# Two low parts made before the last gated columns of each feed-forward layer, and unread products in four waits of the attention layers

## The chip, the core and the metric

The kernel runs on one core of a Trainium2 chip. A core has a matrix engine (TensorE, "PE" in the rows; its weight loads are "PEld"), a vector engine (VectorE, "DVE"), a scalar engine (ScalarE, "ACT"), a general engine (GpSimd, "POOL") and a queue engine (SyncE, "SP") that here only issues transfers. Each engine works through its own list of instructions in order and waits on semaphores that others raise. The metric is the device time of one execution in microseconds (us); lower is better.

## The reference, cut to what matters

A model of twelve layers works on 256 tokens of width 1024, in float32. The layers stand in this order: ffn0, sb (stick-breaking attention), ffn1, ffn2, mla (latent attention), ffn3, ssm, peer0, ple0, swa (windowed attention with shared keys), peer1, ple1. The change touches the four feed-forward layers and the entries of two attentions:

```python
def swiglu(x, w_in, w_out):                    # ffn0 to ffn3
    gate, up = jnp.split(x @ w_in, 2, axis=-1)
    return (jax.nn.silu(gate) * up) @ w_out    # 1024 -> 2816 (gate and up) -> 1024

def multi_head_latent_attention(...):          # mla
    proj = h @ w_in                            # 1024 -> 416
    q = (rms_norm(c_q, q_norm) @ w_uq)         # 256 -> 1536, part of it rotated
    kv = (rms_norm(c_kv, kv_norm) @ w_ukv)     # 128 -> 2048
    ...                                        # causal softmax attention, 16 heads

def swa_sink_attention(...):                   # swa
    q = apply_partial_rope(h @ q_w + q_b, cos, sin)
    ...                                        # windowed softmax attention, 16 heads
```

## The kernel before

**Numbers in two parts.** A float32 product is made of three products of rounded numbers: each operand is split into a high part and a low part (what rounding left over), and `products` (lines 473 to 475) adds high x high, high x low and low x high. The weights come as a stream of blocks of 128 x 1024 numbers into a ring of four places (`ring`, issued on SP's queue, L420). For each block ACT makes the high part (`make_hi`, L310, into `ring_hi`, four slots) and DVE or POOL the low part (`make_lo`, L316, into `ring_lo`). `make_hi` of block b waits until the block has landed and until PE has used block b-4, which had the same slot. The place in the ring is free for block b+4 once the low part of b is made.

**A feed-forward layer** has 66 blocks, numbered here from the layer's first. The hidden width 2816 is 22 columns of 128. For each column c PE multiplies one block of gate and one of up (`up(c)`), ACT takes the silu of the gate (`silu(c)`, L1139), and DVE multiplies and splits it (`hidden(c)`: w_hi L1681, L1682, w_lo L1684). The down blocks of columns 0 to 17 stand among the others. The last six gate and up blocks are 56 to 61, so that `up(21)` is blocks 60 and 61, and the last four down blocks are 62 to 65. They are worked off by `last_row_blocks`: for the first 128 tokens it goes through 62, 63, 64, 65 (six products of 512 columns each), then twice more through all four for the other tokens. Before a block it waits for its low part and for `hidden` of its column (18 to 21). The order on ACT and DVE at this place is written out by hand, and it is the same in all four layers: ACT makes the high parts of 60, 61, 62, then `silu(20)`, then 63, then `silu(21)`, then 64 and 65; DVE makes the low parts of 60 and 61, `hidden(20)`, low part of 62, `hidden(21)`, then the low parts of 63, 64, 65. After the layer `add_normed` (DVE) and `statistics` (ACT) take the sum out of PSUM, norm it and go on to the next layer: each layer begins with the result of the one before.

**Unread products.** `unread_products(n)` (L453) is a row of n float32 products of 128 x 128 with the identity, into an unused corner of PSUM that nobody reads. Before the change it is called with 7 and with 8 in the waits at the entry of the layers (`transposes_of_x`).

**mla** (L720 on): PE multiplies the four blocks of mla_in, then waits for `mla_cn` (ACT copies the product and sums squares, POOL takes the root, DVE scales, L1827); six transposes (L742); a wait for their copy out of PSUM in two parts (ACT L1278, DVE L1833); then 36 products for q, 24 for k and v; a wait for `mla_kv_d` (DVE copies and rotates q, then copies k and v, L1850); then the attention: for every pair of heads a turning of q (L661, in swa L664), scores (L678, L679), softmax on DVE and ACT, a turning of the weights (L688), values (L704). **swa** has the same attention; before it PE turns the keys (L797) and waits for `swa_q` (DVE adds a bias to q and rotates it, L1880).

Of the kernel before, what the change touches and what calls it, by code (L numbers as in the profile page):

```python
# [14 lines left out]
P = 128  # L15
# [5 lines left out]
FC = FF // P  # L21
# [120 lines left out]
def build_program(nc, stream, experts, x_in, pos_in, cols_in, rows_in, out):  # L142
    n_blocks = AT["end"]
    ctx = ExitStack()
    with ctx:
# [287 lines left out]
        def _(pe):  # L433
            ident = col("ident")
# [16 lines left out]
            def unread_products(n):  # L451
                for _ in range(n):
                    pe.matmul(ps[:, 7, 3 * P:4 * P], ident, col("ones"), start=True, stop=True)  # L453
# [270 lines left out]
            def mla():  # L724
# [3 lines left out]
                for k in range(KD):  # L728
                    b = base + k // 2
                    if k % 2 == 0:  # L730
                        wait_split(pe, b)
                    wait_hT(NORM_OF["mla"], k)
                    for tb in range(TB):
                        last = products(ps[:, tb, 0:MLA_IN], h_tiles(k, tb),
                                        ring_parts(b, slice((k % 2) * MLA_IN, (k % 2 + 1) * MLA_IN)),
                                        k == 0, k == KD - 1)
                    if k % 2:
                        last.then_inc(used, 1)
                pe.wait_ge(of("mla_cn"), 1)
# [4 lines left out]
                last.then_inc(of("mla_cT"), 1)  # L744
                pe.wait_ge(of("mla_cTs"), 1)
# [27 lines left out]
                pe.wait_ge(of("mla_kv_a"), 1)  # L773
                pe.wait_ge(of("mla_kv_d"), 1)
                attention(0, R)

            def swa():
# [20 lines left out]
                last.then_inc(of("swa_kT"), 1)  # L798
                pe.wait_ge(of("swa_q"), 1)
# [248 lines left out]
        def _(act):  # L1048
# [83 lines left out]
            def ffn(f, name):  # L1132
# [21 lines left out]
                for c, blocks in ((18, (54, 55, 56)), (19, (57, 58, 59)), (20, (60, 61, 62)), (21, (63,))):  # L1154
                    for b in blocks:
                        make_hi(act, base + b)
                    act.wait_ge(used, base + 3 * FC - TAIL - 2 * (FC - 1 - c) if c > 18 else base + 55)
                    act.wait_ge(hidden_ready, done + c - 1)
                    silu(c).then_inc(silu_ready, 1)
                for b in range(3 * FC - 2, 3 * FC):  # L1160
                    make_hi(act, base + b)
# [386 lines left out]
        def _(dve):  # L1548
# [123 lines left out]
            def ffn(f, name):  # L1672
# [27 lines left out]
                for c, blocks in ((18, (54, 55, 56)), (19, (57, 58, 59)), (20, (60, 61)), (21, (62,))):  # L1700
# [5 lines left out]
                for b in range(3 * FC - 3, 3 * FC):  # L1706
                    make_lo(dve, base + b)
# [678 lines left out]
```

## Time and profile before

| | us |
|---|---|
| median of 3 runs | 2895.51 (2893.81 to 2896.94) |
| the profiled execution, its own time | 2896.59 |
| its span in the trace | 2894.7 |
| PE busy (87% of the span) | 2505.3 |
| DVE busy (60%) | 1727.1 |
| ACT busy (41%) | 1189.8 |
| POOL busy (33%) | 963.2 |

The span is what the trace covers; 1.9 us of the execution lie outside of it. The layers before peer0 take the first 1325 us or so. "Granted clock" is the share of TensorE's full clock that the chip lets through: it is 1.00 (2.4 GHz) or 0.50 (1.2 GHz), and a value between the two is a mean over a stretch that saw both. Matmuls overlap: one of 512 columns lasts 0.39 us in a row of equals, and the next one starts after 0.23 us, so costs are read from starts and not from durations.

### The profile page before, as it was taken

How to read it: one execution, taken by the hardware profiler on the slowest of the kernel's cores; microseconds unless marked ns; L12 is line 12 of the kernel's file. 1: busy time of each engine (PE TensorE's matmuls, PEld its weight loads, DVE VectorE, ACT ScalarE, POOL GpSimd, SP SyncE). 2: the span in 40 equal slices, each digit the busy share in tenths (PEclk: the TensorE clock that was granted, in tenths of full speed). 3: DMA queues.
4: the chain of work that ended last, by engine and by line, in shares of the span. 5: the costliest groups of instructions: out<-in, count | busy, mean ns of one | idle time of the engine just before them, and what ended most of it. 6: DMA issues, size and time to landing. Idle time of an engine off the chain costs nothing.

```text
span 2894.7 us, 35382 instructions
## 1 busy us (share of the span) xinstructions
PE 2505.3 (87%) x12108; PEld 1782.7 (62%) x12108; DVE 1727.1 (60%) x3508; ACT 1189.8 (41%) x2574; POOL 963.2 (33%) x745
## 2 busy tenths in 40 slices
PE   8999899999889999996888787778886888877787
PEld 8988799899769988985444333333664444333334
DVE  5552255655455555785676767665456666676663
ACT  4346543434454356543333322333462333223333
POOL 0015400000320027665544333333534444433343
PEclk9999999999999999998999999999988999999999
DMA  6543255455415544436999999998428999999994
GB/s 210 187 165 124 95 185 192 161 191 180 140 59 182 186 157 139 146 106 241 418 416 419 421 420 418 421 414 331 136 87 362 413 419 418 420 419 417 417 415 182
DMA packets 141957, 783.49 MB, mean 271 GB/s; under 512 B 15872, under 2 KB 16384, under 8 KB 76288
## 3 DMA queue, kind: packets, MB, share of 16 engines
q0 software_dynamic: 73728, 536.90, 44.8%
q1 hardware_dynamic: 65360, 237.44, 24.2%
q10 hardware_dynamic: 2736, 7.46, 0.8%
q8 instruction: 73, 1.20, 0.2%
q14 instruction: 60, 0.49, 0.1%
HBM read 780.69 MB, written 1.05 MB: 270 GB/s over the span
## 4 chain that ended last, share of the span: by engine, by line
PE 47%; DMA 24%; DVE 10%; ACT 7%; issue 7%; POOL 6%; ACTq 0%; POOLq 0%; SPq 0%; DVEq 0%
DMA arena<-experts,arena 23%; PE ps L473 12%; PE ps L474 11%; PE ps L475 11%; PE ps L987 5%; PE ps L990 5%; POOL ring_lo L316 3%; DVE arena L2108 2%; POOL arena L2211 2%; ACT row L1465 2%; ACT arena L1458 1%; ACT L1456 1%; POOL rs L2190 1%; DVE arena L2000 1%; DVE hT_lo L1661 0%
## 5 line engine op out<-in xcount | busy, mean ns | idle before, releaser
L2108 DVE SCALAR_TENSOR_TENSOR arena<-arena,ps 128x1024 f32<-128x1024 f32 x512 | 618.6, 1220 | 430.2 <-DMA arena<-experts,arena 429.8
L987 PE MATMUL ps<-arena,row 128*128 128x512 f32 x1024 | 581.6, 652 | 282.7 <-ACT row L1465 282.7
L2211 POOL DMA_INDIRECT arena<-experts,arena x512 | 483.9, 945 | 683.4 <-PE ps L990 488.5
L473 PE MATMUL ps<-hT_hi,ring_hi 128*128 128x256 f32 x2056 | 590.5, 287 | 11.2 <-DVE hT_lo L1661 8.5
L474 PE MATMUL ps<-hT_lo,ring_hi 128*128 128x256 f32 x2056 | 584.2, 284 | 0.0
L475 PE MATMUL ps<-hT_hi,ring_lo 128*128 128x256 f32 x2056 | 583.8, 284 | 0.0
L990 PE MATMUL ps<-arena,row 128*128 128x512 f32 x1024 | 561.3, 631 | 0.0
L316 POOL TENSOR_TENSOR ring_lo<-ring,ring_hi 128x1024 fp32r<-128x1024 f32 x182 | 450.3, 2486 | 322.8 <-ACT ring_hi L310 247.8
L987 PEld LDWEIGHTS ps<-arena,row 128*128 128x128 f32 x1024 | 200.1, 205 | 572.9 <-ACT row L1465 358.6
L310 ACT ACTIVATE ring_hi<-ring 128x1024 fp32r<-128x1024 f32 x448 | 462.2, 1057 | 105.1 <-PE ps L475 99.0
L473 PEld LDWEIGHTS ps<-hT_hi,ring_hi 128*128 128x128 f32 x2056 | 395.6, 192 | 19.2 <-DVE ring_lo L316 6.1
L474 PEld LDWEIGHTS ps<-hT_lo,ring_hi 128*128 128x128 f32 x2056 | 395.8, 192 | 3.3
L475 PEld LDWEIGHTS ps<-hT_hi,ring_lo 128*128 128x128 f32 x2056 | 395.6, 192 | 0.2
L990 PEld LDWEIGHTS ps<-arena,row 128*128 128x128 f32 x1024 | 209.5, 205 | 274.8 <-issue 274.8
L2190 POOL TENSOR_TENSOR rs<-ms,cols 128x1 f32<-128x1 f32 (+2 forms) x47 | 29.1, 618 | 920.6 <-DVE ms L1578 798.8
L316 DVE TENSOR_TENSOR ring_lo<-ring,ring_hi 128x1024 fp32r<-128x1024 f32 x266 | 311.1, 1220 | 0.2
L1456 ACT ACTIVATE arena<-arena 128x4 f32<-128x4 f32 (+1 forms) x138 | 28.3, 205 | 568.9 <-DVE arena L2108 568.5
L1681 DVE TENSOR_TENSOR w_hi<-ps,arena 128x256 fp32r<-128x256 f32 x88 | 37.4, 425 | 318.1 <-ACT arena L1139 318.1
L1139 ACT ACTIVATE arena<-ps 128x256 f32<-128x256 f32 x88 | 34.0, 387 | 392.6 <-PE ps L475 392.6
L1465 ACT ACTIVATE row<-cols,arena 128x128 f32<-128x128 f32 x512 | 164.7, 390 | 4.5
L473 PE MATMUL ps<-ring_hi,w_hi 128*128 128x512 f32 x352 | 138.4, 393 | 5.9 <-DVE ring_lo L316 5.9
L474 PE MATMUL ps<-ring_lo,w_hi 128*128 128x512 f32 x352 | 137.9, 392 | 0.0
(278 smaller groups left out, 2987.0 us busy)
## 6 DMA issues: line engine op xcount, KB each, us to landing
ring<-stream SPq DMA_DIRECT2D x448, 512.0 KB, 4.2
arena<-experts,arena POOLq DMA_INDIRECT x512, 13.0
row<-rows_in ACTq DMA_DIRECT2D x11, 512.0 KB, 4.7
x<-x_in SPq DMA_DIRECT2D x1, 1024.0 KB, 4.9
out<-arena SPq DMA_DIRECT2D x2, 512.0 KB, 2.6
arena<-cols_in ACTq DMA_DIRECT2D x3, 256.0 KB, 7.2
cols<-cols_in SPq DMA_DIRECT2D x1, 425.5 KB, 5.5
arena<-cols_in ACTq DMA_DIRECT2D x1, 320.0 KB, 2.9
```

The costliest lines, as they stand in the source:

```text
L310: act.activation(ring_hi[:, b % SLOTS, :], ring[:, b % RING, :], ACT.Copy).then_inc(hi_ready, 1)
L316: e.tensor_tensor(ring_lo[:, b % SLOTS, :], ring[:, b % RING, :], ring_hi[:, b % SLOTS, :].bitcast(F32), ALU.subtract).then_inc(lo_ready[w ...
L473: pe.matmul(dst, a[0], b[0], start=start, stop=False)
L474: pe.matmul(dst, a[0], b[1], start=False, stop=False)
L475: return pe.matmul(dst, a[1], b[0], start=False, stop=stop)
L987: lower = pe.matmul(ps[:, 2 * tb, :], diag, v[:, 0:HALF], start=first, stop=end)
L990: pe.matmul(ps[:, 2 * tb + 1, :], diag, v[:, HALF:D], start=first, stop=end)\
L1456: link(act.activation(R["g"][:, n % 2, first:end], R["a"][:, n % 2, first:end], ACT.Gelu))
L1465: last = act.activation(R["diag"][:, k % (2 * GROUP), :], col("ident"), ACT.Copy, scale=R["w"][:, n % 2, k:k + 1])
L2108: last = dve.scalar_tensor_tensor(u, u, 1.0, h, ALU.mult, ALU.mult, accum_out=R["a"][:, n % 2, k:k + 1])
L2190: pool.tensor_tensor(rs[:, a:b], ms[:, a:b], col("nhalf")[:, a:b], ALU.pow).then_inc(rs_ready, 1)
L2211: pool.indirect_dma_start(R["held"][:, g % HELD, :], None, experts, bass.IndirectOffsetOnAxis(ap=idx[:, n % 2, k:k + 1], axis=0))\
```

## The change

In the four feed-forward layers ACT makes the high part of block 64 before `silu(21)` and not after it, and DVE makes the low parts of 63 and 64 before `hidden(21)` and not after it. In mla PE makes 18 unread products before the wait for `mla_cn`, 8 before the wait for `mla_cTs`, and 9 (into bank 3 of PSUM) before the wait for `mla_kv_d`; in swa it makes 20 before the wait for `swa_q`. Nothing is removed.

```diff
@@ -448,9 +448,9 @@
-            def unread_products(n):
+            def unread_products(n, bank_at=7):
                 for _ in range(n):
-                    pe.matmul(ps[:, 7, 3 * P:4 * P], ident, col("ones"), start=True, stop=True)
+                    pe.matmul(ps[:, bank_at, 3 * P:4 * P], ident, col("ones"), start=True, stop=True)
@@ -736,12 +736,14 @@
                     if k % 2:
                         last.then_inc(used, 1)
+                unread_products(18)
                 pe.wait_ge(of("mla_cn"), 1)
                 for c in range(3):
                     for tb in range(TB):
                         last = pe.transpose(ps[:, 2 + c // 2, (c % 2) * T + tb * P:(c % 2) * T + (tb + 1) * P],
                                             R["cn"][:, tb, c * P:(c + 1) * P], ident)
                 last.then_inc(of("mla_cT"), 1)
+                unread_products(8)
                 pe.wait_ge(of("mla_cTs"), 1)
                 pe.wait_ge(of("mla_cTl"), 1)
@@ -771,6 +773,7 @@
                 pe.wait_ge(of("mla_kv_a"), 1)
+                unread_products(9, 3)
                 pe.wait_ge(of("mla_kv_d"), 1)
                 attention(0, R)
@@ -796,6 +799,7 @@
                 last.then_inc(of("swa_kT"), 1)
+                unread_products(20)
                 pe.wait_ge(of("swa_q"), 1)
                 pe.wait_ge(of("swa_kTs"), 1)
                 attention(1, R)
@@ -1151,14 +1155,13 @@
-                for c, blocks in ((18, (54, 55, 56)), (19, (57, 58, 59)), (20, (60, 61, 62)), (21, (63,))):
+                for c, blocks in ((18, (54, 55, 56)), (19, (57, 58, 59)), (20, (60, 61, 62)), (21, (63, 64))):
                     for b in blocks:
                         make_hi(act, base + b)
                     act.wait_ge(used, base + 3 * FC - TAIL - 2 * (FC - 1 - c) if c > 18 else base + 55)
                     act.wait_ge(hidden_ready, done + c - 1)
                     silu(c).then_inc(silu_ready, 1)
-                for b in range(3 * FC - 2, 3 * FC):
-                    make_hi(act, base + b)
+                make_hi(act, base + 3 * FC - 1)
@@ -1697,14 +1700,13 @@
-                for c, blocks in ((18, (54, 55, 56)), (19, (57, 58, 59)), (20, (60, 61)), (21, (62,))):
+                for c, blocks in ((18, (54, 55, 56)), (19, (57, 58, 59)), (20, (60, 61)), (21, (62, 63, 64))):
                     for b in blocks:
                         make_lo(dve, base + b)
                     dve.wait_ge(silu_ready, done + c + 1)
                     dve.wait_ge(used, base + 3 * (c - TAIL) + 5)
                     hidden(c)
-                for b in range(3 * FC - 3, 3 * FC):
-                    make_lo(dve, base + b)
+                make_lo(dve, base + 3 * FC - 1)
                 add_normed(LAYERS.index(name), 0.5)
```

The order of the instructions on DVE at the end of ffn0, before the change: `hidden(20)` is rows 78 to 80, `hidden(21)` rows 82 to 84, and the low parts are the rows of L316.

```order
L1681 TENSOR_TENSOR w_hi<-ps,arena 128x256
L1682 TENSOR_TENSOR arena<-ps,arena 128x256
L1684 TENSOR_TENSOR w_lo<-arena,w_hi 128x256
L316 TENSOR_TENSOR ring_lo<-ring,ring_hi 128x1024
L1681 TENSOR_TENSOR w_hi<-ps,arena 128x256
L1682 TENSOR_TENSOR arena<-ps,arena 128x256
L1684 TENSOR_TENSOR w_lo<-arena,w_hi 128x256
L316 TENSOR_TENSOR ring_lo<-ring,ring_hi 128x1024 x3
```

The same place after the change:

```order
L1684 TENSOR_TENSOR w_hi<-ps,arena 128x256
L1685 TENSOR_TENSOR arena<-ps,arena 128x256
L1687 TENSOR_TENSOR w_lo<-arena,w_hi 128x256
L316 TENSOR_TENSOR ring_lo<-ring,ring_hi 128x1024 x3
L1684 TENSOR_TENSOR w_hi<-ps,arena 128x256
L1685 TENSOR_TENSOR arena<-ps,arena 128x256
L1687 TENSOR_TENSOR w_lo<-arena,w_hi 128x256
L316 TENSOR_TENSOR ring_lo<-ring,ring_hi 128x1024
```

Two of the three low parts that stood behind `hidden(21)` now stand ahead of it. On PE, at the waits of mla (L742 and L743 are the six transposes, L661 the first turnings of q, cT the split input of the 36 and 24 products), the difference is:

```order
-L742 MATMUL ps<-cols,arena 128x128 x6
+L453 MATMUL ps<-cols 128x128 x18
+L743 MATMUL ps<-cols,arena 128x128 x6
+L453 MATMUL ps<-cols 128x128 x8
 L473 MATMUL ps<-ring_hi,cT_at_3663 128x512
 L474 MATMUL ps<-ring_lo,cT_at_3663 128x512
```

The 18 stand ahead of the transposes and the 8 behind them; the 9 and the 20 stand in the same way ahead of the first L661 in mla and the first L664 in swa.

## Rows read from the trace of the kernel before

**Rows 1.** The page of the kernel before: span, and the chain that ended last, by engine.

```profile
span 2894.7 us, 35382 instructions
...
PE 47%; DMA 24%; DVE 10%; ACT 7%; issue 7%; POOL 6%; ACTq 0%; POOLq 0%; SPq 0%; DVEq 0%
```

**Rows 2.** The waits of TensorE: who waited for whom, us in total, times, longest.

```profile
PE ps L473 <- DVE ring_lo L316: 5.9, 4, 1.5
PE ps L664 <- DVE arena L1880: 5.3, 1, 5.3
```

**Rows 3.** Timeline of TensorE at the end of ffn0: start us, us, what.

```profile
191.27 0.40 PE L473 MATMUL ps<-ring_hi,w_hi 128*128 128x512 f32 x1
...
192.43 0.39 PE L475 MATMUL ps<-ring_hi,w_lo 128*128 128x512 f32 x1
194.30 0.50 PE L473 MATMUL ps<-ring_hi,w_hi 128*128 128x512 f32 x1 [1.48 <-DVE ring_lo L316]
...
194.87 0.40 PE L475 MATMUL ps<-ring_hi,w_lo 128*128 128x512 f32 x1
```

**Rows 4.** Timeline of VectorE (DVE), same place.

```profile
181.51 2.36 DVE L316 TENSOR_TENSOR ring_lo<-ring,ring_hi 128x1024 fp32r<-128x1024 f32 x2
...
187.27 1.22 DVE L316 TENSOR_TENSOR ring_lo<-ring,ring_hi 128x1024 fp32r<-128x1024 f32 x1
191.89 0.43 DVE L1681 TENSOR_TENSOR w_hi<-ps,arena 128x256 fp32r<-128x256 f32 x1 [3.40 <-ACT arena L1139]
...
193.03 3.49 DVE L316 TENSOR_TENSOR ring_lo<-ring,ring_hi 128x1024 fp32r<-128x1024 f32 x3
```

**Rows 5.** Timeline of ScalarE (ACT), same place.

```profile
185.71 0.39 ACT L1139 ACTIVATE arena<-ps 128x256 f32<-128x256 f32 x1 [1.76 <-PE ps L475]
...
191.47 0.39 ACT L1139 ACTIVATE arena<-ps 128x256 f32<-128x256 f32 x1 [4.43 <-PE ps L475]
191.75 2.00 ACT L310 ACTIVATE ring_hi<-ring 128x1024 fp32r<-128x1024 f32 x2
```

**Rows 6.** The DMA issues from 165 to 200 us: KB each, median us to landing.

```profile
ring<-stream SPq DMA_DIRECT2D x12, 512.0 KB, 4.4
```

**Rows 7.** Busy us of each engine by stretch, then granted clock (PEclk), DMA share, GB/s.

```profile
212.00:215.40 3.40, 3.40 (x9) 2.60 (x9) 2.36 (x7) 2.74 (x5) 2.58 (x2) 0.52 0.85 348
771.90:785.50 13.60, 6.94 (x19) 5.41 (x20) 6.05 (x23) 2.22 (x5) 5.09 (x3) 0.50 0.38 118
799.20:806.00 6.80, 4.92 (x20) 4.22 (x21) 0.63 (x1) 2.04 (x2) 0.00 (x0) 0.50 0.00 0
2089.50:2106.40 16.90, 12.04 (x52) 7.15 (x53) 12.15 (x34) 9.76 (x31) 0.49 (x1) 0.50 0.00 0
```

**Rows 8.** Timeline of TensorE around and in mla.

```profile
754.86 1.95 PE L453 MATMUL ps<-cols 128*128 128x128 f32 x16
...
775.91 1.54 PE L742 MATMUL ps<-cols,arena 128*128 128x128 f32 x6 [6.67 <-DVE arena L1827]
780.10 0.76 PE L473 MATMUL ps<-ring_hi,cT_at 128*128 128x512 f32 x1 [2.64 <-issue]
...
785.35 0.50 PE L473 MATMUL ps<-ring_hi,cT_at 128*128 128x512 f32 x1
...
799.97 1.91 PE L661 MATMUL ps<-cols,arena 128*96 128x128 f32 x8 [3.11 <-DVE arena L1850]
803.00 1.94 PE L661 MATMUL ps<-cols,arena 128*96 128x128 f32 x8 [1.11 <-ACT arena L1218]
...
806.69 1.04 PE L661 MATMUL ps<-cols,arena 128*96 128x128 f32 x8
```

**Rows 9.** Timeline of TensorE at the entry of the swa attention.

```profile
2092.51 0.69 PE L664 MATMUL ps<-cols,arena 128*128 128x128 f32 x2 [5.34 <-DVE arena L1880]
...
2094.30 0.81 PE L678 MATMUL ps<-arena 64*128 64x128 f32 x4
...
2107.84 0.50 PE L678 MATMUL ps<-arena 64*128 64x128 f32 x4
```

## The prediction, made before the changed kernel was run

> **What bounds the kernel now.** I began with the page's span and its chain of waits [rows 1]. PE holds 47% of the chain, transfers 24%, and no engine is the bound throughout: the layers follow each other, each begins with the result of the one before, and time taken out of one layer's chain moves everything behind it forward by the same amount. So a wait of PE is worth what it stops in its own place. The second view is the list of PE's waits. PE waits for a low part at the end of a feed-forward layer (`ring_lo` L316, 4 times, 1.5 us at most, 5.9 us in total, so once in each of ffn0 to ffn3) and 5.3 us for q of swa (L1880) [rows 2], 6.7 us for the scaled latent of mla (L1827) and 3.1 us for k and v of mla (L1850) [rows 8]. The third view is the timeline at these places, the fourth the granted clock by stretches.
>
> **Part 1, the low parts.** In the trace of ffn0 the tail's first product starts at 191.27, and the sixth at 192.43 [rows 3]: five starts in 1.16 us, 0.232 us each. The seventh, the first of block 63, starts only at 194.30. DVE shows why [rows 4]: it does `hidden(21)` from 191.89, and the low part of 63 is the first third of the group that starts at 193.03 and lasts 3.49 (1.22 each, about 1.15 from start to start), ready at 194.25. The stall is best read from starts: from 192.43 to 194.87 three starts took 2.44 us where three cost 0.70. So 1.74 us lie in the stall, more than the 1.48 which the row calls idle, since durations overlap. Four layers at 1.74 are **7.0 us**.
>
> Does the new order take the whole of it away? A high part takes about 1.0 us, two of them 2.00 [rows 5]. Block 63 has its high part right behind `silu(20)` (185.71, lasts 0.39), at about 186 to 187.1, so its low part follows that of 62 (187.27, ends 188.5) and is ready at about 189.7. For block 64 ACT must wait until PE has used block 60. The two silus stand at 185.71 and 191.47 [rows 5], each at the end of two column blocks, so a block takes 2.88 us, and block 60 is used at about 188.6. The high part lasts to 189.7, the low part, 1.22, to 190.9. `hidden(21)` starts at 191.89, and is not delayed: 1.0 us of room on DVE, and on ACT 1.8 us up to `silu(21)`. The block must have landed by 188.6. Its transfer is issued when the low part of 60 is made, the first of the two that start at 181.51 [rows 4], about 182.7, and lands in 4.4 us [rows 6], at 187.1: 1.5 us of room. SP's queue gets its next releases earlier, never later, and the later blocks of the stream only gain.
>
> What is late next? Without the stall PE reaches block 64 at 191.27 + 12 x 0.232 = 194.1 (low part at 190.9, `hidden(20)` long done), and block 65 at 191.27 + 18 x 0.232 = 195.4. For 65 it needs `hidden(21)`, ready at 193.1, and the one low part left on DVE, ready at 194.3. 1.1 us of room, so nothing replaces the stall. Bounds of this part: 5.9 (the rows' idle alone) and 7.0; I take 7.0, since it is counted from starts. Behind the tail ACT and DVE wait for PE, so the gain goes on.
>
> **Part 2, the unread products, as work.** Sixteen of them last 1.95 us at full clock [rows 8], so 0.11 to 0.12 each from start to start; at half clock the six transposes of the same size last 1.54, or 0.22 each. The 18 take 2.0 us at full and 4.0 at half clock, in a wait of 6.67. The 8 take 1.8 at half clock; between the transposes' end (777.45) and the next start (780.10) lie 2.64. The 9 take 1.0 to 2.0 in a wait of 3.1, the 20 take 2.2 to 4.4 in a wait of 5.3 [rows 8, 9]. All end before what PE waits for. As work they cost nothing, and what hides them is the chain on ACT, POOL and DVE, which doesn't need PE. If that cover were gone they would cost their own length, 7.0 us at most for the 55 at full clock less what still hides them.
>
> **Part 2, the unread products, for the clock.** In the waits the clock falls: it is 0.50 from 771.9 to 785.5, from 799.2 to 806.0, and from 2089.5 to 2106.4 [rows 7]. What does that cost? First, the six transposes: at full clock 6 x 0.12 and one tail, 0.85 and not 1.54: 0.7. Then the dense products: twelve starts from 780.10 to 785.35 took 5.25 us where they cost 2.8: 2.45. The DVE chain that leads to the attention (copy of q, rotation, k and v) hangs on the end of these products, so both go on. At the entry of the attention two turnings of q last 1.91 and 1.94 where one at full clock lasts 1.04 [rows 8], with ACT's copies in series between them: 1.75, and some 0.4 for the first scores: 2.1. In swa a turning is 0.25 longer (0.69 for two transposes), a group of scores 0.3 in L678 alone (0.81 for 0.50) [rows 9], about 0.7 with the products behind it; two of each stand in the chain before DVE is the bound: 2.0 at most. The whole prize is 3.15 + 2.1 + 2.0 = 7.3 us.
>
> How much of it is won? Nothing that I have says it exactly, so I bound it. Below: nothing in each, as the clock still falls in each wait. Above: all. A loss is excluded for the clock itself, since added work can't make a fall come earlier. The nearest rows are the two falls: in the first wait the clock fell 2.7 us after PE went idle (idle from 775.91 - 6.67 = 769.24, fall at 771.9), in the second 2.3 us after (from 799.97 - 3.11 = 796.86 to 799.2). The 18 leave 4.7 us of idle, clearly more: it falls, later. I give that wait nothing by itself. The 8 fill 1.8 of the 2.64 us behind the transposes. In the trace the clock came back only after 5.25 us of nearly unbroken work, which began at 780.10; with the 8, work is nearly unbroken from 775.9, and the climb may come 0 to 4 us earlier. I take 1.2, half of the 2.45. The 9 leave 2.1 us of idle, a little less than either, but gaps of 1.1 us follow between the turnings: half of 2.1, 1.0. The 20 leave 3.1 us, which is more than both: it falls, and I take 0.2. Sum **2.4 us**, between 0 and 7.3.
>
> A page weighs this otherwise. The rows count a loss only where PE's own products stood in the chain: in the 13.6 us stretch PE was busy for 6.94, and half of its waits would be as long at full clock. The Trainium skill, "TensorE: Matmul & The Clock Gate", section "Terms", estimates the penalty of a stretch at half clock as its length times one half, whatever PE does in it. That would be an estimate of 18.7 us for the 37.3 us of the three stretches instead of 7.3; the busy time in the rows speaks against it.
>
> **The sum.** 7.0 + 2.4 = 9.4 us off the profiled execution's own 2896.6 (span 2894.7 and 1.9 around it) gives 2887.2. That execution was 1.1 above the median of the runs, which gives 2886.1.
>
> **The rivals.**
> *The clock gives nothing.* It falls in each wait and comes back at the same place, as the 4.7 and 3.1 us of idle suggest, and the 2.1 us with gaps behind it may be enough too. Then only part 1 counts: 2888.5. A small variant of the same: falls of the clock aren't tied to a place. From 212.0 to 215.4, PE busy 3.40 of 3.40 us, it was at 0.52 [rows 7], worth 1.7 us. One such fall more or less is in every execution, and my range holds it.
> *The clock stays full throughout.* All 7.3 are won: 2881.2. For it speaks that idle of 1.5 us in the tails left it at full; against it the 4.7 us. By the rule of half the stretch it would be 18.7 us, 2869.8 (the page named above); I give that 1 in 100.
> *The stall moves.* Block 64 is late by more than its room, or PE waits for 65 or for the transfer, and most of the 7.0 comes back at the next block: 1 us or so saved in the tails, and 1.5 by the clock, 2893. This is also the case in which the change doesn't do what it says: the low part of 64 is not there ahead.
> *Slower: ACT and DVE are held by block 64.* Now ACT waits for the landing of 64 and for the use of 60 with `silu(21)` queued behind it, and DVE waits for the high part with `hidden(21)` queued behind it; PE waits for both. If 64 landed later than 188.6 by d, `hidden(21)` is free until d = 1.0, PE until d is about 2.1, and the 1.74 is used up at d = 3.9. Above that each us costs 1 us in each layer. With d = 5.5, a transfer of 11 us and not 4.4, each layer loses 1.6, less 1 by the clock: 2901. The median of the landings speaks against it.
>
> **How the numbers follow.** Forecast 0.68, 2886.1, its own range 2883.5 to 2889. Clock gives nothing 0.12; full clock 0.06, half of the stretch 0.01; stall moves 0.10; held by block 64 0.03. Less than 0.2% (5.8 us, bound 2889.7) is about what a measurement of this kernel can't tell from no change. Faster by more: nearly all of the forecast and of the full-clock cases, and most of the clock-gives-nothing case, together 0.85; within 0.2%: 0.12; slower: 0.03. The range goes from 2882 to 2890: it holds the forecast, the case without any help of the clock with its noise of 1.5 us, and most of what lies towards full clock, and leaves out the last three cases.
>
> **What would show it.** In the list of waits of the changed kernel the row of L473 for `ring_lo` by DVE with 4 times is gone, and the tail of ffn0 shows starts 0.23 us apart across blocks 62 to 65; DVE shows three low parts in a row ahead of the last `hidden`, and `hidden(21)` starts within 0.1 us of the silu as before. If it starts late, block 64 holds DVE. In mla the clock falls later than 2.7 us after the last product of mla_in, the transposes behind that wait last 0.85 (full) or 1.54 (half), and the clock is back less than 9.6 us after them. The first two turnings of q last 1.04 (full) or 1.91 (half). In swa I expect the turnings at half clock, 0.69, as before. The prediction is wrong if tails without the stall give less than 6 us, or if the clock gives more than 5.

## The result, and the profile after

The changed kernel took 2882.09 us (median of 5 runs, 2877.25 to 2885.01), the kernel before 2895.51 in the same comparison. The ratio is 0.9947, with a 95% interval from 0.9936 to 0.9958: 12 to 19 us less, where 9.4 had been forecast. The same kernel, compared once more on another occasion (e8, below), gave 0.9966 (0.9953 to 0.9979), 6 to 14 us less. The two together say about 0.9957, some 12.5 us. So the direction was right and the size too small: 9.4 is three quarters of 12.5. A good part of this document is about where the rest comes from, and why the two comparisons of one kernel differ. "x us less" is here and below the ratio applied to the time before; the difference of the two medians can be 1 to 2 us off it (13.4 us here, 10.0 in e8). The median of 2882.09 stands at the low edge of the forecast range (2882 to 2890), and by the ratio the gain of 15.4 us lies past that edge, which is 13.5 below the kernel before.

The page of the profiled execution after (its own time 2878.12 us), span and chain by engine:

```profile
span 2876.3 us, 35601 instructions
...
PE 47%; DMA 23%; DVE 10%; issue 7%; ACT 6%; POOL 6%; ACTq 0%; POOLq 0%; DVEq 0%; SPq 0%
```

The waits of TensorE after, against [rows 2]:

```profile
PE ps L743 <- DVE arena L1829: 2.7, 1, 2.7
...
PE ps L661 <- DVE arena L1852: 1.0, 1, 1.0
PE ps L473 <- POOL ring_lo L316: 1.0, 2, 0.7
...
PE ps L664 <- DVE arena L1882: 0.9, 1, 0.9
```

The row of L473 for `ring_lo` by DVE, 5.9 us in [rows 2], is gone; the one by POOL (1.0 us) belongs to other layers and was there before. The waits of mla and swa have become short: 2.7 us at L743 (6.67 at L742 in [rows 8]), 1.0 at L661 (3.1), 0.9 at L664 (5.3).

The end of ffn0. TensorE, against [rows 3] (start us, duration us): the last product of block 62, the first of 63, of the second half of 63, and of 64.

```profile
190.47 0.39 PE L475 MATMUL ps<-ring_hi,w_lo 128*128 128x512 f32 x1
190.70 0.39 PE L473 MATMUL ps<-ring_hi,w_hi 128*128 128x512 f32 x1
...
191.38 0.39 PE L473 MATMUL ps<-ring_hi,w_hi 128*128 128x512 f32 x1
...
192.06 0.39 PE L473 MATMUL ps<-ring_hi,w_hi 128*128 128x512 f32 x1
```

VectorE and ScalarE in the same place, against [rows 4] and [rows 5]: the three low parts (the first line), the one left over, the high part of 64, `silu(21)`.

```profile
185.30 3.71 DVE L316 TENSOR_TENSOR ring_lo<-ring,ring_hi 128x1024 fp32r<-128x1024 f32 x3
...
191.06 1.22 DVE L316 TENSOR_TENSOR ring_lo<-ring,ring_hi 128x1024 fp32r<-128x1024 f32 x1
```

```profile
186.69 1.06 ACT L310 ACTIVATE ring_hi<-ring 128x1024 fp32r<-128x1024 f32 x1 [1.61 <-PE ps L475]
189.51 0.38 ACT L1143 ACTIVATE arena<-ps 128x256 f32<-128x256 f32 x1 [1.76 <-PE ps L475]
```

The starts are 0.23 us apart across the blocks. The high part of 64 starts at 186.69, 2.8 us ahead of `silu(21)`, and the three low parts end at 189.0, before `hidden(21)` can start (189.93, 0.42 behind its silu as before).

The unread products and what follows them, TensorE, against [rows 8] and [rows 9]:

```profile
760.33 4.18 PE L453 MATMUL ps<-cols 128*128 128x128 f32 x36
767.22 1.54 PE L743 MATMUL ps<-cols,arena 128*128 128x128 f32 x6 [2.71 <-DVE arena L1829]
768.56 2.81 PE L453 MATMUL ps<-cols 128*128 128x128 f32 x16
...
785.54 2.17 PE L453 MATMUL ps<-cols 128*128 128x128 f32 x18
788.71 1.08 PE L661 MATMUL ps<-cols,arena 128*96 128x128 f32 x8 [1.01 <-DVE arena L1852]
```

```profile
2072.10 4.63 PE L453 MATMUL ps<-cols 128*128 128x128 f32 x40
2077.61 0.44 PE L664 MATMUL ps<-cols,arena 128*128 128x128 f32 x2 [0.88 <-DVE arena L1882]
```

This is the row on which the forecast broke. Eighteen products are x36, and last 4.18 us; twenty are x40 and last 4.63. The last record alone lasts 0.28, so the 36 start 0.112 us apart, and a product, which has two records, takes 0.223 us from start to start. The busy time and the granted clock by stretches, against [rows 7] (us, PE, PEld, DVE, ACT, POOL busy, then PEclk, DMA share, GB/s):

```profile
766.90:770.30 3.40, 3.08 (x15) 3.08 (x16) 0.53 (x3) 1.20 (x3) 2.35 (x1) 0.50 0.29 101
770.30:790.70 20.40, 18.44 (x95) 15.09 (x94) 11.48 (x32) 5.33 (x5) 2.41 (x1) 1.00 0.15 52
790.80:794.20 3.40, 3.29 (x14) 3.05 (x15) 0.00 (x0) 1.07 (x2) 0.00 (x0) 0.50 0.00 0
2072.10:2110.00 37.90, 24.39 (x198) 16.82 (x196) 33.93 (x85) 29.12 (x96) 10.07 (x4) 1.00 0.17 56
2110.00:2140.00 30.00, 27.94 (x144) 22.23 (x145) 10.15 (x20) 9.55 (x16) 10.15 (x5) 1.00 0.21 71
```

Half clock in mla is down from 20.4 us to 6.8, and in swa, where it had been 16.9 us at the entry and 6.8 later, it is gone in this execution.

To see where the time went I cut each trace at the first low part of hT of every layer (the line of `norm_in` on DVE, L1661 in the kernel before; for swa the same line writes the low part of oT). The lengths in us, each from one profiled execution, worked out from the starts of these instructions:

| stage | before | after | tails only (e1) | after again (e8) | too many (e7) | e11 |
|---|---|---|---|---|---|---|
| ffn0 | 198.48 | 194.81 | 196.82 | 194.82 | 194.81 | 196.71 |
| sb | 154.85 | 153.44 | 153.35 | 153.03 | 153.42 | 153.26 |
| ffn1 | 196.56 | 194.80 | 194.80 | 194.80 | 194.81 | 194.81 |
| ffn2 | 196.60 | 194.83 | 194.82 | 194.83 | 194.82 | 194.83 |
| mla | 113.98 | 110.71 | 114.07 | 111.47 | 113.26 | 110.66 |
| ffn3 | 198.07 | 194.80 | 194.80 | 194.80 | 194.80 | 196.28 |
| swa | 103.22 | 98.99 | 104.32 | 99.88 | 106.69 | 104.11 |
| the rest | 1732.9 | 1733.9 | 1735.1 | 1738.2 | 1737.1 | 1737.0 |

In ffn1 and ffn2 the change is the same to 0.03 us in every trace with the whole new order: 1.77 us, the tail. ffn0 and ffn3 hold the same 1.77 and something more that is not always there.

### The profile page after: what moved, and what is told of

Its sections match the earlier page's. It is cut to its first block, busy times and chain, and to the rows that moved or that the text cites. A ratio compares the mean times of both kernels' runs of the same rounds, so it can differ in the third digit from the quotient of the medians.

```text
span 2876.3 us, 35601 instructions
## 1 busy us (share of the span) xinstructions
PE 2505.8 (87%) x12218; PEld 1786.6 (62%) x12218; DVE 1729.8 (60%) x3508; ACT 1190.2 (41%) x2574; POOL 964.3 (34%) x745
## 4 chain that ended last, share of the span: by engine, by line
PE 47%; DMA 23%; DVE 10%; issue 7%; ACT 6%; POOL 6%; ACTq 0%; POOLq 0%; DVEq 0%; SPq 0%
DMA arena<-experts,arena 23%; PE ps L473 12%; PE ps L474 12%; PE ps L475 12%; PE ps L991 5%; PE ps L994 5%; POOL ring_lo L316 3%; DVE arena L2110 2%; POOL arena L2213 2%; ACT row L1468 2%; ACT arena L1461 1%; ACT L1459 1%; POOL rs L2192 1%; DVE arena L2002 1%; DVE hT_lo L1664 0%
## 5 line engine op out<-in xcount | busy, mean ns | idle before, releaser
L473 PE MATMUL ps<-hT_hi,ring_hi 128*128 128x256 f32 x2056 | 588.9, 286 | 11.2 <-DVE hT_lo L1664 8.5
L316 POOL TENSOR_TENSOR ring_lo<-ring,ring_hi 128x1024 fp32r<-128x1024 f32 x182 | 451.1, 2491 | 313.2 <-ACT ring_hi L310 238.4
L473 PEld LDWEIGHTS ps<-hT_hi,ring_hi 128*128 128x128 f32 x2056 | 393.9, 192 | 19.2 <-DVE ring_lo L316 6.1
L316 DVE TENSOR_TENSOR ring_lo<-ring,ring_hi 128x1024 fp32r<-128x1024 f32 x266 | 311.5, 1219 | 0.7
L473 PE MATMUL ps<-ring_hi,w_hi 128*128 128x512 f32 x352 | 137.9, 392 | 0.0
```

What stands on the lines that cost most here:

```text
L316: e.tensor_tensor(ring_lo[:, b % SLOTS, :], ring[:, b % RING, :], ring_hi[:, b % SLOTS, :].bitcast(F32), ALU.subtract).then_inc(lo_ready[w ...
L473: pe.matmul(dst, a[0], b[0], start=start, stop=False)
```

## The experiments

All times are medians of a kernel, beside the kernel before run together with it; ratios have 95% intervals. e1 to e4 ran together, then e5 to e8, then e9 to e12.

### e1 and e2: the two parts apart

e1 is the changed kernel without the added products:

```diff
-                unread_products(18)
-                unread_products(8)
-                unread_products(9, 3)
-                unread_products(20)
```

> The changed kernel without its 55 added products: only the order at the four ends of ffn0 to ffn3 is new. My theory: each tail is 1.75 us shorter and nothing else changes, so 7.0 us less than the kernel before (ratio 0.9976), and the mla and swa entries are as slow as before (36 to 39 us from the last product of mla_in to the third turning; first turnings in swa 0.69). Rival: the order is worth more than its own stall, since the whole came out 13 to 15 us faster against the 9.4 forecast; then this kernel alone is 10 us or more faster.

Measured: 2888.69 us against 2897.04, 0.9975 (0.9966 to 0.9984), 7.2 us less, 4.6 to 9.8 by the interval. ffn1 and ffn2 are 1.77 us shorter each, mla and swa as long as before (114.07 and 104.32). The theory holds, the rival falls: the order is worth its own stall, 4 x 1.77 = 7.1 us.

e2 is the changed kernel with the old order in the tails:

```diff
-                for c, blocks in ((18, (54, 55, 56)), (19, (57, 58, 59)), (20, (60, 61, 62)), (21, (63, 64))):
+                for c, blocks in ((18, (54, 55, 56)), (19, (57, 58, 59)), (20, (60, 61, 62)), (21, (63,))):
...
-                for c, blocks in ((18, (54, 55, 56)), (19, (57, 58, 59)), (20, (60, 61)), (21, (62, 63, 64))):
+                for c, blocks in ((18, (54, 55, 56)), (19, (57, 58, 59)), (20, (60, 61)), (21, (62,))):
```

The two loops behind these lines go back to the old order with them, so that the high parts of 64 and 65 and the low parts of 63 to 65 are made there.

> The changed kernel with the old order in the tails; all 55 products are in. Theory formed from the changed kernel's trace, where 18 products last 4.18 us (x36 records) and not the 2.0 I had reckoned (I had read x16 as sixteen products; they are eight): the products fill the waits to 2.7, 0 to 0.9, 1.0 and 0.9 us, the clock stays up, and mla gives 3.4 us and swa 1.8 to 2.2: 5.5 us less than before (ratio 0.9981). Rival: the products give the 2.4 us of the prediction and the rest of the gain was falls of the clock that happened to be missing elsewhere; then ratio 0.9992.

Measured: 2891.87 against 2897.04, 0.9983 (0.9972 to 0.9995), 4.9 us less. The interval holds 5.5, and with 1.4 to 8.1 us it also holds 2.4: the time alone leaves the rival standing. The stages tell more: mla 110.84, swa 99.82, 3.1 and 3.4 us shorter than in the trace of before. The parts add up: 7.2 + 4.9 = 12.1, against some 12.5 for both.

### e3 and e4: the products of mla and of swa apart

e3 is e2 without the 20 products of swa; e4 is e2 without the 18, 8 and 9 of mla. The edit of e3 beyond e2:

```diff
-                unread_products(20)
```

> Old tails, no products in swa: only the 18, 8 and 9 of mla. Theory: 3.4 us less than before (0.9988); the profile shows mla about 3.3 us shorter from the entry of mla to its attention, and swa as before. Rival (the prediction's sum): 2.2 us. The time alone may not tell these; the length of the stage in the trace does.

> Old tails, no products in mla: only the 20 of swa. Theory: the 20 last 4.6 us and leave 0.9, the clock stays at full through the entry of the attention, and swa is 1.8 to 2.2 us shorter up to the first weights (0.9993), up to 4 if a later fall in the same attention goes too. Rival (the prediction): 0.2 us.

Measured: e3 2895.65, 0.9993 (0.9984 to 1.0002); e4 2894.19, 0.9993 (0.9984 to 1.0002); 2.0 us less each, and neither is told from no change by its time. In the traces mla of e3 is 111.43 (114.0 before), swa of e4 99.78 (103.2 before). In e3 swa has no products and is 102.11, in e1 104.32, in the kernel before 103.22: 2 us of difference without any difference in the code. So single stages of single executions must be taken as draws, and the means over all traces are below.

### e5: half as many products

```diff
-                unread_products(18)
+                unread_products(9)
-                unread_products(8)
+                unread_products(4)
-                unread_products(9, 3)
+                unread_products(4, 3)
-                unread_products(20)
+                unread_products(10)
```

> The changed kernel with 9, 4, 4 and 10 products for 18, 8, 9 and 20, so that they last about as long as the prediction had reckoned (2.1, 0.9, 0.9, 2.3 us), tails as changed. If the only failed step was the length of a product, this one does what the prediction said: 7.0 from the tails and about 2.4 from the clock, 9.4 less than before (0.9968), with the swa turnings at half clock. Rival: even half of them keeps the clock up, then it is as fast as the changed kernel (12.5 or more, 0.9957 or less).

Measured: 2887.04 against 2895.68, 0.9967 (0.9955 to 0.9980), 9.6 us less (5.8 to 13.0 by the interval). TensorE at the entry of the swa attention:

```profile
2076.95 2.40 PE L453 MATMUL ps<-cols 128*128 128x128 f32 x20
2082.46 0.44 PE L664 MATMUL ps<-cols,arena 128*128 128x128 f32 x2 [3.11 <-DVE arena L1882]
2083.37 0.69 PE L664 MATMUL ps<-cols,arena 128*128 128x128 f32 x2 [0.47 <-ACT arena L1223]
```

Ten products last 2.40 us, 3.11 us of idle are left, and the second turning is at half clock (0.69): swa takes 104.14 us, as without any. In mla half as many do as well as all (110.72 in this trace). So the interval doesn't prove that e5 is slower than the changed kernel; the swa stage says why it should be. The 9.6 us agree with the 9.4 of the forecast, which had products of this length in mind, but the interval is wide, and the parts don't match theirs: by the stages it is 7.1 for the tails, 3.0 for mla where the forecast had 2.2, and nothing for swa.

### e6: only block 63 ahead

The added products are out here too; of the tails:

```diff
-                for c, blocks in ((18, (54, 55, 56)), (19, (57, 58, 59)), (20, (60, 61, 62)), (21, (63, 64))):
+                for c, blocks in ((18, (54, 55, 56)), (19, (57, 58, 59)), (20, (60, 61, 62)), (21, (63,))):
...
-                for c, blocks in ((18, (54, 55, 56)), (19, (57, 58, 59)), (20, (60, 61)), (21, (62, 63, 64))):
+                for c, blocks in ((18, (54, 55, 56)), (19, (57, 58, 59)), (20, (60, 61)), (21, (62, 63))):
```

The loops behind these lines make 64 and 65.

> No products. In the tails only the low part of block 63 stands ahead of the last gated column; the high and low parts of 64 and 65 stay behind it. PE then reaches 64 at 194.1 on the old clock of ffn0, and its low part is ready at 194.3 (first behind the hidden step): theory: the stall shrinks to 0.1 to 0.4 us a layer, so 5.5 to 6.5 us less than before. Rival: a restart costs its full price wherever it stands, then less than 5 us.

Measured: 2890.07 against 2895.68, 0.9981 (0.9969 to 0.9994), 5.5 us less. ffn1 takes 195.20 us: 1.37 of the 1.77 are won, 4 x 1.37 = 5.5 (the interval is 1.7 to 9.0). The stall that is left, 0.4 us, stands one block later, at the first product of 64. That is the second half of what the change does: the low part of 64 ahead is worth 0.4 us a layer.

### e7: too many products

```diff
-                unread_products(18)
+                unread_products(36)
-                unread_products(20)
+                unread_products(40)
```

> The changed kernel with 36 and 40 products for 18 and 20 (8 and 9 as they are). The cover ends: 36 at 0.235 us are 8.5 us in a wait of 6.7, and 40 are 9.3 in a wait of 5.5. Theory: the transposes start at once behind them, 1.8 us later, and the swa turnings 3.8 us later; the clock gains 0.7 in the transposes and 1 to 2 in what follows. In sum 3 to 5 us slower than the changed kernel. Rival (0.117 us each, as predicted): 4.2 and 4.7 us long, no cost.

Measured: 2891.11 against 2895.68, 0.9983 (0.9974 to 0.9992); 4.9 us slower than the changed kernel run beside it (e8, 0.9966), though the two intervals overlap a little. TensorE in mla and at the entry of the swa attention:

```profile
760.33 8.20 PE L453 MATMUL ps<-cols 128*128 128x128 f32 x72
768.37 0.82 PE L743 MATMUL ps<-cols,arena 128*128 128x128 f32 x6
...
2078.83 9.10 PE L453 MATMUL ps<-cols 128*128 128x128 f32 x80
2087.76 0.38 PE L664 MATMUL ps<-cols,arena 128*128 128x128 f32 x2
```

36 last 8.20 us and 40 last 9.10 (0.23 each with the end of the last); no wait is left in front of the transposes (L743) or of the turning (L664), both start as the products end. The transposes take 0.82 us and not 1.54: full clock. mla comes out at 113.26, 2 us longer than with 18, swa at 106.69, some 6 longer than with 20. Not all of this is the overrun. Up to the first masked scores on DVE mla is 1.1 us longer than in the traces whose entry is at full clock like this one (43.80 against 42.67 in e2 and 42.68 in e9), and swa 3.4 longer than with 20. The rest stands late in the stages, behind the last scores, where half clock from 75 to 85 us into mla and again late in swa costs 3.7 us each against traces without it. So the cover was real, and it ends where the length of 0.23 says; at 0.12 both rows would have ended inside their waits (6.7 and 5.5 us).

### e8: the changed kernel again

> The changed kernel itself once more, to see which stages differ from one execution to the next. Theory: tails 1.77 each, mla 3.3, swa 1.8 or more shorter again; the 1.9 us at the start, 1.7 at the entry of sb and 1.5 in ffn3 by which the first trace was shorter differ from execution to execution and come with falls of the clock. Median 2882 to 2884. Rival: those 5 us are there again, and belong to the change.

Measured: 2885.72 against 2895.68, 0.9966 (0.9953 to 0.9979). Tails, mla (111.47) and swa (99.88) are short as in the first trace, and so are ffn0, sb and ffn3; but ssm and peer0 are 4.7 us longer between them, with the same code. The median is 2 us above what I expected. What, then, made the first trace of the changed kernel 18.4 us shorter than that of the kernel before? Beside the tails, mla and swa it is three stretches. In ffn0 it is the first climb of the clock. No granted clock is on record in the first 12 us, so the starts tell it. TensorE at 14.7 us, before and after:

```profile
14.70 0.41 PE L473 MATMUL ps<-hT_hi,ring_hi 128*128 128x256 f32 x1
14.91 0.41 PE L474 MATMUL ps<-hT_lo,ring_hi 128*128 128x256 f32 x1
```

```profile
14.71 0.28 PE L473 MATMUL ps<-hT_hi,ring_hi 128*128 128x256 f32 x1
14.83 0.28 PE L474 MATMUL ps<-hT_lo,ring_hi 128*128 128x256 f32 x1
```

0.21 us from start to start in the kernel before, 0.12 after; the first full clock is on record at 17.6 and at 12.6 us. Over all fourteen traces the climb came at 11.7 to 12.9 in eight (after, e2, e4, e7, e8, e9, e10, e12) and at 16.8 to 18.2 in six (before, e1, e3, e5, e6, e11), with ffn0 1.6 to 2.2 us longer in these six. It isn't tied to the change: it lies ahead of the first instruction that was moved, e1 has the late climb with the new tails, and e4 the early one with the old. In sb (154.7 to 154.9 or 153.0 to 153.4) and ffn3 (197.9 to 198.1 or 196.6 with the old tail) it is one fall of 3.4 us at the entry that is there or not. These two are less free of the change than they look. In sb the fall stands in three of the four traces with the old tails (before, e3, e4, not e2) and in none of the ten with blocks moved ahead; in ffn3 it stands in the same three and, of the ten, in e11 alone.

### e9 to e12: how full, and which wait of mla

Four counts, tails as changed, against 18, 8, 9 and 20: e9 has 26, 10, 11, 22; e10 18, 0, 0, 15; e11 0, 8, 0, 20; e12 0, 0, 9, 5. The edit of e9:

```diff
-                unread_products(18)
+                unread_products(26)
-                unread_products(8)
+                unread_products(10)
-                unread_products(9, 3)
+                unread_products(11, 3)
-                unread_products(20)
+                unread_products(22)
```

> Tails as changed, and 26, 10, 11 and 22 products for 18, 8, 9 and 20, so that at 0.235 us each they fill the waits nearly whole (6.1 of 6.7, 2.4 of 2.6, 2.6 of 3.1, 5.2 of 5.5 us). Theory: in mla the short fall that the changed kernel still has goes too, and mla is 110.0 us or less from its entry to ffn3 where the changed kernel has 110.7 to 111.5; swa 99.6 as with 20. Sum 0 to 1.5 us faster than the changed kernel. Rival: if the clock falls all the same, products at half clock (0.45 each) overrun the second wait (4.5 of 2.6) and it is up to 2 us slower.

Measured: 2884.41 against 2896.53, 0.9959 (0.9947 to 0.9971). Busy time and granted clock of mla and of a later stretch in swa:

```profile
760.00:800.00 40.00, 35.80 (x231) 30.94 (x230) 20.86 (x49) 17.78 (x39) 10.65 (x6) 1.00 0.22 75
2111.80:2121.90 10.10, 8.05 (x36) 5.07 (x36) 3.92 (x10) 1.69 (x3) 0.00 (x0) 0.50 0.01 2
```

The clock is at full throughout mla, which takes 108.44 us, the shortest of all traces: the last short falls are gone. But swa has half clock from 2111.8 to 2121.9, at the end of its attention, and 102.78 us. In sum the intervals don't tell it from the changed kernel.

> Tails as changed; of mla's products only the 18 of the first wait; 15 in swa for 20. Question: which of the three waits of mla carries the 2.6 us. Theory: the 18 alone leave the second wait open, so the clock falls and comes back only in the dense products: 0 to 1 us, mla at 112.7 to 113.7 (113.7 is the mean without products). In swa 15 last 3.5 us and leave 2.0: the turnings are at full clock, swa 99 to 101. Rival for swa: 2.0 us are too long, then 103 to 104.

Measured: 2886.85 against 2896.53, 0.9968 (0.9953 to 0.9983). mla 114.04: the 18 alone give nothing, as supposed (one trace; the forecast of 112.7 to 113.7 is just missed). swa with 15 is 98.99: with 2.0 us of idle left the turnings are still at full clock.

> Tails as changed; of mla's products only the 8 behind the transposes; swa as changed. Theory: they start the climb 2.6 us earlier, so the dense products are at full clock sooner: 1 to 2 us, mla at 112 to 112.7; the two first turnings of the attention stay at half clock. In swa again 98.9 to 99.9, and no late fall before the output projection ends (four of four profiles with the 20, none of six without). If the late fall is there, it is not the 20 that take it away.

Measured: 2885.18 against 2896.53, 0.9964 (0.9954 to 0.9974). mla 110.66 in the one trace: the 8 alone give 3.0 us, as much as all three in the first trace of the changed kernel (110.72), and more than the 1 to 2 I expected. TensorE behind the transposes:

```profile
769.18 1.54 PE L742 MATMUL ps<-cols,arena 128*128 128x128 f32 x6 [6.68 <-DVE arena L1827]
770.51 2.71 PE L453 MATMUL ps<-cols 128*128 128x128 f32 x16
```

The products start at half clock right behind the transposes; the clock is back at 772.1, 2.9 us after the transposes began, and the dense products that had lost 2.45 us are all at full clock. The other claim fell. Busy time and granted clock at the entry of the swa attention and at its end:

```profile
2079.00:2093.00 14.00, 9.82 (x79) 7.50 (x77) 10.82 (x28) 6.53 (x22) 0.00 (x0) 1.00 0.01 1
2113.60:2130.50 16.90, 13.37 (x57) 8.74 (x56) 8.36 (x21) 5.04 (x16) 0.00 (x0) 0.50 0.03 12
```

Full clock at the entry as always with the 20, but half clock for 17 us from 2113.6 on, and swa takes 104.11 us. The late fall is not what the 20 take away.

> Tails as changed; of mla's products only the 9 ahead of the attention; 5 in swa for 20. Theory: the first turnings of q last 1.05 or one of them 1.5; 1 to 2 us, mla at 112 to 112.7. In swa 5 last 1.2 us of 5.5 and do nothing: 103 to 104.5, late fall there.

Measured: 2888.89 against 2896.53, 0.9966 (0.9955 to 0.9977). The entry of the mla attention is shorter (the two first turnings last 1.08 and 1.50, and the first scores come 0.8 us sooner than in before), but the stage is 115.83, as a fall stands later in it. swa 103.08, as without products. The stage theory for mla (112 to 112.7) missed.

## Why the prediction was right or wrong

Means over the traces, with the kernels that have a part and those that have not:

| part | without | with | difference | forecast |
|---|---|---|---|---|
| one tail (ffn1, ffn2) | 196.58 (before, e2, e3, e4) | 194.81 (after, e1, e5, e7 to e12) | 1.77, four times 7.1 | 7.0 |
| mla | 113.7 (before, e1, e4, e6) | 111.1 (after, e2, e3, e8) | 2.6 | 2.2 |
| swa | 103.5 (before, e1, e3, e6) | 100.5 (after, e2, e4, e8, e11) | 3.0 | 0.2 |
| sum | | | 12.7 | 9.4 |

Nearly all of the 3.3 us between the sums is swa's 2.8.

mla and swa can be cut further, at the first and the last masked scores on DVE (`arena<-ps,arena` 128x768, L1784 in the kernel before). Means over the same traces, in us:

| piece | without | with | difference |
|---|---|---|---|
| mla, entry to first scores | 47.95 | 44.08 | 3.9 |
| mla, first to last scores | 27.14 | 27.14 | 0 |
| mla, behind the last scores | 38.62 | 39.89 | -1.3 |
| swa, entry to first scores | 35.96 | 34.74 | 1.2 |
| swa, first to last scores | 26.96 | 26.98 | 0 |
| swa, behind the last scores | 40.58 | 38.80 | 1.8 |

**Part 1, the low parts: right.** 1.77 us a layer for a forecast 1.74, read from starts across the stall. The 1.48 in the wait's row would have given 5.9 where e1 has 7.2. The room that was reckoned for block 64 was there: its high part ran 186.69 to 187.75, 2.8 us ahead of `silu(21)`, and `hidden(21)` was not held. The next thing late, block 65, was not late. Shown by e1 (the part alone) and e6 (half of it).

**The length of a product: wrong, the step that failed.** "Sixteen of them last 1.95 us at full clock" read the x16 of L453 in [rows 8] as sixteen products. But the code ahead of it calls `unread_products(8)`: the trace has two records for each float32 product, and one for each transpose of the same size (x6 for six at L742). A product costs 0.223 us from start to start at full clock and not 0.12. The wait rows and the counts in the code together would have shown it. The Trainium skill, "FP8 and Floating Point Precision", section "TensorE Precision Notes", says that true float32 takes four passes through the array; at 128 columns and 2.4 GHz that is an estimate of 0.21 us a product. The measured 0.223 is close to it, and twice what I used; the trace shows two records for a product and not four. What followed from the mistake: the idle left in the waits was 2.7, about 0, 1.0 and 0.9 us and not 4.7, 0.9, 2.1 and 3.1. That as work they cost nothing stayed true, with less to spare than was written; e7 shows where it ends.

**The clock in mla: right in size, by luck in part.** 2.2 forecast, 2.6 measured, but the 2.6 is a sum of two things that the forecast didn't have so. The entry gained 3.9 on the mean, and in e2 and e9 5.3, all of the prize of 5.25 that was reckoned for it. Behind the last scores 1.3 went back: a fall of the clock that begins 73 to 78 us into the stage stands in five of the nine traces with the 8 or the 9 (e2, e3, e7, e8, e12), and in none of the five without them (before, e1, e4, e6, e10). The prediction excluded a loss by the clock, "since added work can't make a fall come earlier"; these traces speak against that, though no run shows what makes the late fall. Of the single terms, nothing for the 18 by themselves is borne out by e10 (114.04). The 8 bring the climb forward, as said, but they carry the full 2.45 of the dense products and the rest of a total of 3.0 in e11, where half was taken. The 9 bring about 0.8 at the entry (e12) for a forecast 1.0. Halving all of them took nothing away (e5, 110.72), so the failed length did little harm here. With no half clock left in the stage, mla is 5.5 us shorter (e9) for the 20.4 us that it had before, about half of what half the stretch would be.

**The clock in swa: wrong, the term that was mis-sized.** 0.2 forecast, 3.0 measured. Two reasons. The first is the length: with ten products, 2.4 us long, there is no gain (e5, 104.14), as the forecast says for 3.1 us of idle; with fifteen to twenty-two the entry is at full clock in all seven traces that have them. With the entry at full clock the first masked scores come 1.2 us sooner (39.50 to 39.52 us after the first low part of hT for the keys in all seven, against 40.73 in before), inside the 2.0 that the prediction gave as its bound. The second is a stretch that the bound left out. Between the first and the last scores nothing is gained on the mean, 27.0 us either way. The half clock of the kernel before reached 10 us into them, but in five of the seven the clock fell again 4 to 6 us behind the first masked scores (e2, e4, e8, e9, e11), and with no half clock at all this piece is only 0.6 us shorter (26.45 in after and e10): DVE is the bound there, as the prediction said. The other 1.8 us lie behind the last scores. That piece takes 37.8 us in the five traces without a late stretch at half clock, and 39.2 to 42.8 in the nine that have it. It is there in all six traces with ten products or fewer, in the one with forty (e7), and in two of the seven with fifteen to twenty-two (e9, e11). So only the 1.2 us are shown to be the work of the 20 products. What decides the late stretch isn't settled, as I have no run that moves it alone, and the 3.0 is a mean over draws from 98.99 to 104.11 us with the same 20.

**The rest of the first comparison.** The two traces differ by 1.9 us more in ffn0, 1.4 in sb and 1.5 in ffn3. The 1.9 is not the change's. Whether the falls in sb and ffn3 have to do with the old tails is open: they stand in three of four traces with them and hardly in the others, but code and work are alike where they fall, and the medians of e1 (7.2) and e6 (5.5) leave nothing beyond the tails' own 7.1 and 5.5, within intervals of 2.6 us and more to each side. The prediction knew of such falls (it named one worth 1.7 us) but gave them 1.5 us in the range; the two comparisons of one kernel came out 5.5 us apart by their ratios and 3.6 by their medians, with intervals that overlap.

**The rivals.** Clock gives nothing: fell (e2, and the entries of mla and swa). Full clock throughout: nearest to what happened in the first trace, 14 us by its sum where 18.4 were between the spans; half the stretch, 26 us, never seen. The stall moves: didn't happen; e6 shows the form it takes with one block ahead, 0.4 us a layer. Held by block 64: didn't happen.

## What to carry to other kernels

Before an instruction is priced from a trace row, count it against the code: a row's x can count passes and not instructions, and a factor of two in a filler's length decides what idle is left. Price a stall from the starts on both sides of it and not from the idle that the row names. Where a clock that falls after idle is at stake, fill the wait in which the dense work follows (8 products of 55 carried mla), up to but not past the end of the wait, and judge by several traces by stage and by piece of a stage: the kernel before alone ran from 2889.6 to 2902.7 us in one comparison. A stage's total can hide a gain at its entry and a loss at its end.

## What the runs showed of the hardware

A float32 product of 128 x 128 has two records and takes 0.223 us from start to start at full clock (18 in 4.18 us), a transpose of the same size one record and 0.11 (six in 0.82 us, e7). The first climb to full clock in an execution comes at one of two places, 11.7 to 12.9 or 16.8 to 18.2 us after the start, and the later one costs 1.6 to 2.2 us. Nearly unbroken work that began with six transposes stood ahead of a climb 2.9 us after they began (e11), where 9.6 us had passed in the kernel before. And full clock gained at one place can come with a fall at a later one: a fall 73 to 78 us into mla stands only in traces with the 8 or the 9 products (five of nine), where it costs 1.3 to 3.7 us. Half clock costs little where DVE is the bound: the eight masked scores of swa start over 26.9 to 27.3 us with 8 to 14 us of half clock among them, and over 26.45 without any (after, e10).
